# A hybrid trunk on one core: the first norm's small inputs, its row of weights and its PSUM banks

## What is computed

```
inv_freq = ROPE_THETA ** (-jnp.arange(0, HEAD_DIM, 2) / HEAD_DIM)
ang = positions[..., None] * inv_freq            # cos and sin of it turn q and k
...
h = rms_norm(x, mix_norm[l])                     # x * rsqrt(mean(x * x) + eps) * g
z = h @ w_in[l]                                  # 1024 x 5632
u, q, k, v, g_ssm, g_attn = jnp.split(z, SPLITS, axis=-1)
```

## Time and profile before

| | us |
|---|---|
| three runs, median (lowest, highest) | 1545.47 (1544.84, 1548.14) |
| the profiled execution | 1546.55 |
| its span, first to last instruction | 1544.8 |
| PE busy | 1489.7 (96%) |
| PEld busy | 1259.2 (82%) |
| DVE busy | 1216.4 (79%) |
| ACT busy | 901.7 (58%) |
| POOL busy | 72.7 (5%) |
| moved by DMA | 393.59 MB, mean 255 GB/s |

### The profile page before, as it was taken

How to read it: one execution, slowest core, us unless ns; L and a number is a source line. 1 busy time by engine, 2 the same in 40 slices (tenths; PEclk the granted TensorE clock), 3 DMA queues, 4 the chain that set the end, 5 groups by cost and what they waited for, 6 DMA issues and landing times.

```text
span 1544.8 us, 23733 instructions
## 1 busy us (share of the span) xinstructions
PE 1489.7 (96%) x8991; PEld 1259.2 (82%) x8991; DVE 1216.4 (79%) x1291; ACT 901.7 (58%) x882; POOL 72.7 (5%) x114
## 2 busy tenths in 40 slices
PE   4899999999999999997999999999999999999997
PEld 4688877999988888886788888888888888888886
DVE  5988876576455787865988989879888798898986
ACT  5234653433334346634677767767677677776774
POOL 0810100000000000101000000000000000000000
PEclk9999999999999999999999999999999999999999
DMA  6254345454364442452998998989989889899894
GB/s 254 72 198 164 127 148 202 178 191 164 91 219 168 174 164 79 157 202 99 377 364 320 375 356 320 364 324 362 351 323 377 337 343 349 324 374 353 312 371 165
DMA packets 77359, 393.59 MB, mean 255 GB/s; under 512 B 28528, under 2 KB 28656, under 8 KB 30448
## 3 DMA queue, kind: packets, MB, share of 16 engines
q1 hardware_dynamic: 75392, 391.28, 67.4%
q10 hardware_dynamic: 1904, 1.43, 0.3%
HBM read 388.88 MB, written 1.05 MB: 252 GB/s over the span
## 4 chain that ended last, share of the span: by engine, by line
PE 83%; DVE 7%; SPq 3%; ACT 2%; issue 2%; DMA 2%; DVEq 0%; ACTq 0%; POOL 0%; POOLq 0%
PE psum L1681 25%; PE psum L1683 25%; PE psum L1682 24%; PE psum L1697 3%; SPq L637 3%; PE psum L1985 2%; DVE w_lo L551 2%; ACT w_hi L545 1%; SPq L646 1%; PE psum L1703 1%; DMA w_raw<-in_stream 1%; DMA rows<-in_rows 1%; PE psum L1795 1%; PE psum L1732 0%; PE psum L2003 0%
## 5 line engine op out<-in xcount | busy, mean ns | idle before, releaser
L551 DVE TENSOR_TENSOR w_lo<-w_raw,w_hi 128x2048 fp32r<-128x2048 f32 x270 | 614.4, 2290 | 160.1 <-ACT w_hi L545 158.0
L545 ACT ACTIVATE w_hi<-w_raw 128x2048 fp32r<-128x2048 f32 x270 | 513.7, 1913 | 304.5 <-PE psum L1683 251.4
L1681 PE MATMUL psum<-w_hi,hsT_hi 128*128 128x512 f32 (+1 forms) x512 | 188.4, 368 | 1.6 <-issue 1.6
L1683 PE MATMUL psum<-w_lo,hsT_hi 128*128 128x512 f32 (+1 forms) x512 | 187.0, 365 | 0.0
L1682 PE MATMUL psum<-w_hi,hsT_lo 128*128 128x512 f32 (+1 forms) x512 | 186.8, 365 | 0.0
L1681 PE MATMUL psum<-w_hi,hT_hi 128*128 128x512 f32 x384 | 156.1, 407 | 7.5 <-DVE w_lo L551 7.3
L1683 PE MATMUL psum<-w_lo,hT_hi 128*128 128x512 f32 x384 | 151.4, 394 | 0.0
L1682 PE MATMUL psum<-w_hi,hT_lo 128*128 128x512 f32 x384 | 151.2, 394 | 0.0
L551 DVE TENSOR_TENSOR w_lo_more<-w_raw,w_hi_more 128x2048 fp32r<-128x2048 f32 x56 | 128.1, 2287 | 26.5 <-ACT w_hi_more L545 26.5
L1681 PE MATMUL psum<-hT_hi,w_hi 128*128 128x256 f32 x416 | 119.4, 287 | 2.7 <-DVE act_ff L1453 2.7
L1682 PE MATMUL psum<-hT_hi,w_lo 128*128 128x256 f32 x416 | 118.8, 286 | 0.0
(11 more groups left out here) (383 smaller groups left out, 2755.8 us busy)
## 6 DMA issues: line engine op xcount, KB each, us to landing
w_raw<-in_stream SPq DMA_DIRECT2D x326, 1024.0 KB, 6.5
w_raw_more<-in_stream SPq DMA_DIRECT2D x40, 1024.0 KB, 7.2
gain_row<-in_gain_rows SPq DMA_DIRECT2D x3, 512.0 KB, 5.8
x_tok<-in_x SPq DMA_DIRECT2D x1, 1024.0 KB, 5.2
uT_lags<-uT_by_lag SPq DMA_DIRECT2D x64, 16.0 KB, 1.9
zT_by_lag<-uT_lags SPq DMA_DIRECT2D x64, 16.0 KB, 1.8
out_trunk<-out_tok SPq DMA_DIRECT2D x2, 512.0 KB, 2.6
s_direct<-s_direct_lags SPq DMA_DIRECT2D x40, 16.0 KB, 2.0
```

Of the source, the lines that this page charges most:

```text
L545: nc.scalar.activation(split_of(seg, i)[0], raw_of(seg, i), ACT.Copy).then_inc(s_hi, 1)
L551: nc.vector.tensor_tensor(l_, raw_of(seg, i), h.bitcast(F32), ALU.subtract).then_inc(s_lo, 1)
L1681: mm(out, lh, rh, start=start, stop=False)
L1683: return mm(out, lh, rl, start=False, stop=stop)
```

## The change

- The positions (as the bits of their integers) and the 32 frequencies become 34 more values in the columns' array, which grows from 138 to 172 per partition; their two transfers and the semaphore s_set are gone, and `angles` waits for the columns.
- ScalarE issues the row of norm weights first, and only into partition 0 (4 KB); columns and lambda rows follow. POOL writes a tile of ones first of all. TensorE multiplies a row of ones by the gain row, in two products of 512 columns, into banks 6 and 7, and the first norm reads its weights there (`norm` with n = 0). The other norms load the row as before.
- In the first norm the four groups of transposes write banks 4, 5, 2 and 3, and no group waits for a bank. ScalarE takes them in the order 0, 2, 1, 3, that of VectorE.

```diff
--- before.py
+++ after.py
@@ -120,6 +120,8 @@
     ("lam_im", DEPTH * PAIRS, lambda a: by_chunk(a["ssm_lambda_im"], PAIRS)),
     ("log_dt", DEPTH * PAIRS, lambda a: np.repeat(a["ssm_log_dt"].reshape(DEPTH, PAIRS, 2).transpose(2, 0, 1), STATE, 0)),
     ("subln", DEPTH, lambda a: a["subln"].transpose(1, 0)),
+    ("positions", NT, lambda a: np.ascontiguousarray(a["positions"].reshape(NT, P).transpose(1, 0)).view(np.float32)),
+    ("inv_freq", HD // 2, lambda a: np.repeat(inv_freq(), P, 0)),
 ]
 COL_AT = {n: sum(k for _, k, _ in COLUMN_ARRAYS[:i]) for i, (n, _, _) in enumerate(COLUMN_ARRAYS)}
 COLUMNS = sum(k for _, k, _ in COLUMN_ARRAYS)
@@ -248,6 +250,7 @@
         s5fr = sb("s5_fr", [P, DEPTH, PAIRS])
         s5fi = sb("s5_fi", [P, DEPTH, PAIRS])
         stat = sb("norm_stat", [P, 4])
+        onerow = sb("one_row", [P, P])
         mean = sb("norm_mean", [P, 4])
         rstd = sb("norm_rstd", [P, 4])
         mx = sb("score_max", [P, 4])
@@ -389,14 +392,14 @@
             sp_[0] += size(shape, dt)
             return at(name, shape, dt, a)
 
-        posi = su("positions_int", [P, NT], I32)
+        posi = cols[:, COL_AT["positions"]:COL_AT["positions"] + NT].bitcast(I32)
         posf = su("positions_f", [P, NT])
         ang = su("angle", [P, NT * 32 + DEPTH * PAIRS])
         angk = su("angle_turns", [P, NT * 32 + DEPTH * PAIRS])
         angr = su("angle_rest", [P, NT * 32 + DEPTH * PAIRS])
-        rows_ = su("rows", [P, 4 * DEPTH * HD + HD // 2])
+        rows_ = su("rows", [P, 4 * DEPTH * HD])
         lamv = rows_[:, 0:4 * DEPTH * HD].rearrange("p (n l d) -> p n l d", n=4, l=DEPTH)
-        invf = rows_[:, 4 * DEPTH * HD:]
+        invf = cols[:, COL_AT["inv_freq"]:COL_AT["inv_freq"] + HD // 2]
         lamp = su("lambda_prod", [P, 2, DEPTH, HD])
         lams = su("lambda_sum", [P, 2, DEPTH])
         lame = su("lambda_exp", [P, 2, DEPTH])
@@ -417,7 +420,7 @@
 
         s_raw = [sem(f"raw_landed{p}") for p in range(NR)]
         s_hi, s_lo, s_used = sem("w_hi_ready"), sem("w_lo_ready"), sem("w_used")
-        s_x0, s_set, s_cols, s_c, s_b = sem("x_landed"), sem("rows_landed"), sem("columns_landed"), sem("c_landed"), sem("b_landed")
+        s_x0, s_cols, s_c, s_b = sem("x_landed"), sem("columns_landed"), sem("c_landed"), sem("b_landed")
         s_lam = sem("lambda_rows_landed")
         s_gf, s_rw, s_out = sem("final_gain_landed"), sem("router_landed"), sem("out_stored")
         s_pool, s_dve, s_actc = sem("pool_step"), sem("dve_step"), sem("act_step")
@@ -446,6 +449,7 @@
         s_rwh, s_rwl = sem("router_w_hi_ready"), sem("router_w_lo_ready")
         s_S, s_ysh, s_ysl, s_scat, s_scatv = sem("select_ready"), sem("y_hi_ready"), sem("y_lo_ready"), sem("scattered"), sem("scatter_taken")
         s_fin = sem("out_ready")
+        s_one, s_grow = sem("one_row_ready"), sem("first_gain_spread")
         s_w4, s_turn = sem("block_turn_ready"), sem("turns_ready")
 
 
@@ -495,6 +499,12 @@
 
         def gate_bank(j):
             return 6
+
+        def norm_bank(l, which, g):
+
+            if (l, which) == (0, 0):
+                return (4, 5, 2, 3)[g]
+            return 4 + TR_AT[l, ("h1", "h2")[which], g] % 2
 
         def freed(n, r=None):
 
@@ -727,6 +737,7 @@
             own = Own(pool, s_pool)
 
 
+            nc.gpsimd.memset(onerow[:, :], 1.0).then_inc(s_one, 1)
             own.do(nc.gpsimd.memset(ident[:, :], 0.0))
             own.do(nc.gpsimd.memset(maskb[:, :], 0.0))
             own.settle()
@@ -789,11 +800,9 @@
         @block.scalar
         def _(act):
             own = Own(act, s_actc)
+            act.dma_start(grow[0:1, :], t["gain_rows"][0:1, :]).then_inc(s_gr, 16)
             act.dma_start(cols[:, :], t["columns"]).then_inc(s_cols, 16)
-            act.dma_start(posi[:, :], t["positions"]).then_inc(s_set, 16)
-            act.dma_start(invf, t["rows"][:, 4 * DEPTH * HD:].to_broadcast([P, HD // 2])).then_inc(s_set, 16)
-            act.dma_start(grow[:, :], t["gain_rows"][0:1, :].to_broadcast([P, D])).then_inc(s_gr, 16)
-            act.dma_start(rows_[:, 0:4 * DEPTH * HD], t["rows"][:, 0:4 * DEPTH * HD].to_broadcast([P, 4 * DEPTH * HD])).then_inc(s_lam, 16)
+            act.dma_start(rows_[:, :], t["rows"].to_broadcast([P, 4 * DEPTH * HD])).then_inc(s_lam, 16)
 
             def norm_sums(ready=None, final=False):
 
@@ -809,12 +818,12 @@
 
             def norm_hi(l, which):
 
-                for g in range(4):
+                for g in (0, 2, 1, 3) if (l, which) == (0, 0) else range(4):
                     n = TR_AT[l, ("h1", "h2")[which], g]
                     q, kh = g // 2, g % 2
                     act.wait_ge(s_tr, n + 1)
                     nc.scalar.activation(hTh[:, 4 * kh:4 * kh + 4, q * P:(q + 1) * P],
-                                         bank(4 + n % 2).rearrange("p (k n) -> p k n", n=P), ACT.Copy).then_inc(s_thi, 1)
+                                         bank(norm_bank(l, which, g)).rearrange("p (k n) -> p k n", n=P), ACT.Copy).then_inc(s_thi, 1)
 
             def trig():
 
@@ -1036,21 +1045,21 @@
 
                 dve.wait_ge(s_rstd, NT * n + q + 1)
                 if q == 0:
-                    dve.wait_ge(s_gr, 16 * (n + 1))
+                    dve.wait_ge(*((s_gr, 16 * (n + 1)) if n else (s_grow, 2)))
                 for kh in halves:
                     cs = slice(kh * 512, (kh + 1) * 512)
-                    V.scalar_tensor_tensor(xn[:, q, cs], x[:, q, cs], rstd[:, q:q + 1], grow[:, cs],
+                    V.scalar_tensor_tensor(xn[:, q, cs], x[:, q, cs], rstd[:, q:q + 1], grow[:, cs] if n else bank(6 + kh),
                                            ALU.mult, ALU.mult).then_inc(s_xn, 1)
 
 
             def angles():
 
-                dve.wait_ge(s_set, 32)
+                dve.wait_ge(s_cols, 16)
                 NA = NT * 32
-                own.do(V.tensor_copy(posf[:, :], posi[:, :]))
+                own.do(V.tensor_copy(posf[:, :], posi))
                 own.settle()
                 for q in range(NT):
-                    own.do(V.tensor_scalar(ang[:, q * 32:(q + 1) * 32], invf[:, :], posf[:, q:q + 1], None, ALU.mult))
+                    own.do(V.tensor_scalar(ang[:, q * 32:(q + 1) * 32], invf, posf[:, q:q + 1], None, ALU.mult))
                 dve.wait_ge(s_dt, 1)
                 own.do(V.tensor_tensor(ang[:, NA:].rearrange("p (l q) -> p l q", l=DEPTH), lim[:, :, :], dtt[:, :, :], ALU.mult))
                 V.tensor_tensor(q1[:, :, :], lre[:, :, :], dtt[:, :, :], ALU.mult).then_inc(s_q1, 1)
@@ -1219,9 +1228,9 @@
 
                 n = TR_AT[l, ("h1", "h2")[which], g]
                 q, kh = g // 2, g % 2
-                dve.wait_ge(s_thi, thi[0] + g + 1)
+                dve.wait_ge(s_thi, thi[0] + ((0, 2, 1, 3).index(g) if (l, which) == (0, 0) else g) + 1)
                 at_ = (slice(None), slice(4 * kh, 4 * kh + 4), slice(q * P, (q + 1) * P))
-                V.tensor_tensor(hTl[at_], bank(4 + n % 2).rearrange("p (k n) -> p k n", n=P), hTh[at_].bitcast(F32),
+                V.tensor_tensor(hTl[at_], bank(norm_bank(l, which, g)).rearrange("p (k n) -> p k n", n=P), hTh[at_].bitcast(F32),
                                 ALU.subtract).then_inc(s_trf[n % 2], 1)
 
             def norm_tail(l, which):
@@ -1706,7 +1715,7 @@
 
                 for g in range(4):
                     q, kh = g // 2, g % 2
-                    b = tr_bank(TR_AT[l, name, g])
+                    b = tr_bank(TR_AT[l, name, g]) if n else bank(norm_bank(0, 0, g))
                     if n:
                         idle_products((0, 0, (0, 44, 24, 52)[n], 12)[g])
                     pe.wait_ge(s_xn, 4 * n + g + 1)
@@ -1825,6 +1834,10 @@
                 else:
                     pe.wait_ge(s_accV, ACCV_L * l + 2 * sum(1 for k in range(b) if k not in EVAC_BY_ACT) + q + 1)
 
+            pe.wait_ge(s_one, 1)
+            pe.wait_ge(s_gr, 16)
+            for c in range(2):
+                mm(bank(6 + c), onerow[0:1, :], grow[0:1, c * 512:(c + 1) * 512], start=True, stop=True).then_inc(s_grow, 1)
             pe.wait_ge(s_const, 1)
             for l in range(DEPTH):
                 seg = 2 * l
@@ -2139,10 +2152,9 @@
 
 INPUTS = {
     "x": lambda a: a["x"].reshape(SEQ, D),
-    "positions": lambda a: a["positions"].reshape(NT, P).transpose(1, 0),
     "columns": lambda a: np.concatenate([lay(a).reshape(P, -1) for _, _, lay in COLUMN_ARRAYS], 1),
     "rows": lambda a: np.concatenate([a["lambda_q1"].reshape(1, -1), a["lambda_k1"].reshape(1, -1),
-                                      a["lambda_q2"].reshape(1, -1), a["lambda_k2"].reshape(1, -1), inv_freq()], 1),
+                                      a["lambda_q2"].reshape(1, -1), a["lambda_k2"].reshape(1, -1)], 1),
     "s5_b": lambda a: np.stack([a[n].reshape(DEPTH, PAIRS, 2, STATE, GCH).transpose(0, 2, 3, 1, 4)
                                 .reshape(DEPTH, P, PAIRS, GCH) for n in ("ssm_b_re", "ssm_b_im")], 2),
```

## The result

The changed kernel takes **1532.48 us** (median of 4, 1531.12 to 1535.56) against 1545.58 for the kernel before in the same comparison: ratio 0.992, 95% interval 0.9907 to 0.9932, so 13.1 us (10.5 to 14.4). The direction was forecast, the amount was not: 1537.2 was said, with 1534.0 as the low end. Its profiled execution took 1532.64 us (span 1530.9).

What follows compares the result with a forecast made beforehand. VectorE was taken to bound the kernel up to 63.4 us, with TensorE waiting for its w_lo. 3.3 us (columns) plus 5.0 us (banks and order) made 8.3 us, giving 1537.2 us, range 1534.0 to 1541.2.

Steps and rivals of the forecast that it cites:

- Bound, place, and what passes on: Between 31.6 and 63.4 us VectorE bounds and TensorE waits; moving the third w_lo (31.55) forward moves the w_lo at 61.11.
- Edit 1: Start: positions and frequencies ride in the columns' array, landing at 7.5; first norm at 10.5 for 13.86, 3.3 us earlier.
- Rivals a and b: Columns' landing: a, mixed with x_tok, at 4.1, 1535.0 us, chance 0.17; b, sharing with weights, at 10.3, 1540.0, chance 0.15.
- The rule of the Trainium skill weighed in the prediction: At the start: each DMA engine goes round between queues with work, so the columns would get their turn within x_tok.
- Edit 2: Before the first norm: gain row by two TensorE products, about 1.9 us, done before 6, hidden under the columns' wait.
- Edit 3: First norm to third w_hi: four banks and ScalarE's order 0, 2, 1, 3 bring the third w_lo 5.0 us forward.
- What is late next: TensorE's early work ends at 34.9, its w_lo comes at 38.0: still VectorE bound, 3 us in hand.
- as the earlier trace had let fear: First half block: products at 415 ns instead of 282 could cost 5.1 us and give back up to 2; nothing taken.
- the sum: Whole kernel: 3.3 us from the columns plus 5.0 from banks and order make 8.3 us, giving 1537.2.
- what would make it wrong: Gain at the third w_lo but not at 61.11, or columns' landing less 7.5 not passing one for one into the time.

Runs made afterwards that it cites:

- columns_first: The changed kernel with the columns issued ahead of the gain row: 1531.17 us, ratio 0.9913.
- run 229: Not a run's label: "run" is a verb here, 1704 products run 229 to 230 instead of 233 ns apart.
- moved_640: The kernel before with only 640 unused bytes per partition ahead of norm_mean: 1540.18 us, ratio 0.9977.
- old_places: The changed kernel with columns and one_row at the top of SBUF and a hole where the columns were, other tiles as before: 1537.39 us, ratio 0.9949.
- all_640: The kernel before with 640 unused bytes ahead of the first tile, x_tok, so everything lies higher: 1544.57 us, ratio 0.9993.
- moved_192: The kernel before with 192 unused bytes ahead of norm_mean: 1535.81 us, ratio 0.993.
- two_banks: The changed kernel with transposes back in two banks and ScalarE's order 0, 1, 2, 3: 1535.81 us, ratio 0.9941.

## Why the prediction was right and wrong

- **Bound, place, and what passes on: right.** TensorE waited for VectorE's w_lo from the start up to 63 us, and a microsecond at the third w_lo is one at 61.11 (9.33 and 9.37).
- **Edit 1: mechanism right, size 0.8 off.** The columns landed at 6.69, not 7.5; the angles took their 3.0 us from there, so 4.15 for 3.3. x_tok landed at 5.9 (issued at 0.78, 5.1 us) where 5.5 was said, and the columns 0.8 behind it where 1.5 and 0.55 had been added. The landing moves from one execution to the next (6.7, 7.3, 7.4 and 7.7 in the four kernels with the same head of the queue), so 7.5 was a fair value and its spread of 1 us should have stood in the range. Rivals a and b fell: between 3.5 and 5 us the ScalarE queue moved no packet, and the first packet of the columns started at 5.03, as x_tok's were running out (the last started at 5.21). DMA packets of the changed kernel by queue, first in 3.5:5, then in 5:6:

```profile
q1 hardware_dynamic: 152, 0.62, 101.2%
...
q1 hardware_dynamic: 63, 0.33, 80.0%
q10 hardware_dynamic: 131, 0.09, 27.6%
```

  The rule of the Trainium skill weighed in the prediction ("DMA: Bandwidth & Descriptors", "Queues, rings and completion order") fails for the columns too, as it did for the positions: issued at 1.34, they moved none of their 128 packets before 5.03.
- **Edit 2: hidden, as said, but its price was wrong.** Not 1.9 us but 3.75, at a granted clock of 1.00: the trace shows four products of 512 columns for the two in the program. It ended at 6.06 under the wait for the columns. In columns_first, where that cover is gone, it sets the norm's start. The Trainium skill, "FP8 and Floating Point Precision", "TensorE Precision Notes", says that true FP32 goes through the array in four passes; the trace shows two instructions for each product and cannot tell passes within one.
- **Edit 3: right.** 5.0 was said, 5.18 measured here and 5.10 alone. The transposes came in one piece of 3.30 us (3.6 said), w_hi of tile 1 at 5.17 after the norm (5.2), its w_lo at 7.23 (7.5), the third w_lo at 12.51 (12.7).
- **What is late next: nothing, as taken.** TensorE was slow for a while, as the earlier trace rows had let fear: after some 2 us without work it began at 15.88 with products of 0.28 us, from 16.8 to 20.0 they took 0.41 at a granted clock of 0.50 (1.2 GHz), then 0.28 again. 18 products in 3.20 us, which follow each other at 0.12 on either side, are 1.0 us lost. It still waited 2.38 us for the w_lo before 36.99, where 3 had been counted on, and VectorE stayed the bound.
- **The step that failed is the sum**, "3.3 + 5.0 = 8.3 us": it took the three edits for all that the change does, and the steady part after 63 us for untouched, since its instructions are the same ones in the same order. A term was missing: the tile one_row and the 34 columns move all tiles behind norm_mean by 640 bytes against w_hi and w_lo, and 1704 products run 229 to 230 instead of 233 ns apart, less what other pairs lose, about 4 us. With the start as measured, 9.35, and 4.2 from moved_640, the sum is 13.5; measured were 13.1. Without it, old_places, the kernel takes 1537.4, the forecast's 1537.2 by a hair, and that is partly luck: the kernel before took 1544.35 in that comparison and not 1545.5, and the gain was 7.0 where 8.3 had been forecast.
- None of the things named under "what would make it wrong" happened; the sign by which the miss shows is one that I had not listed: a lead that grows after 63 us.

## What to carry to other kernels

Compare the lead of the changed kernel at several points along the span, not at the end alone: a lead that grows where the instructions are the same is no part of the edit's mechanism. A new or widened SBUF tile changes the distance between all tiles behind it and those ahead of it; before crediting or blaming an edit for a few tenths of a per cent, run the kernel before with an empty hole of that size. And where a kernel is bound by products, try such holes on purpose: here one line with 128 or 192 bytes gave 3.5 and 9.4 us. The distance to try first for products of 512 columns is a multiple of 256 bytes between the two operands' tiles, the best in all the kernels here; for those of 256 columns it was not.

## What the hardware showed that I had not expected

The time between two products of 512 columns depends on the distance in SBUF between the tile that TensorE loads (here the state's) and the tile that it passes through (here the weights'): 233, 233, 230 and 227 ns at 64, 128, 192 and 256 bytes past a multiple of 512, at the same granted clock. The Trainium skill, "TensorE: Matmul & The Clock Gate", "Step-by-step: what each phase is for", says that TensorE has two independent read ports into SBUF and that loading the next weights (its word for the loaded operand) takes no read bandwidth from the running product. By that the distance should not matter; the all_640 run against moved_640 says that it does, by 3 to 4 ns in 230, and moved_192 by 6. What inside the chip makes it is open: no run measured a load apart from a product.

How far the period is settled: that a shift of 512 changes nothing rests on two pairs of runs (128 and 640, 192 and 704). That 256 is a period too rests on one other pair of tiles, w_hi_more with eactT, whose steps at 320, 384 and 448 are those of hsT at 64, 128 and 192; no run put hsT itself there. Open are distances that are no multiple of 64 and why products of 256 columns go another way. The distance is also not all: w_hi_more with hsT, which keep theirs, change from 228.6 to 229.4 ns with 640 bytes.

The surplus of two_banks, some 6 us where 4.2 were due, needs no cause of its own: its interval holds both, its profile shows 3.4, and its products have the steps of distance 192.
